# The last expert tile added to the residual on TensorE in PSUM, and the second-last tile's down products moved forward

## The reference

```python
x = x + mixer(rmsnorm(x))
lg = u @ router_group_w + b      # top-1 of 4 groups
le = u @ router_expert_w + b     # top-2 of the 4 experts of that group
h = silu(u @ expert_w_gate) * (u @ expert_w_up)      # 1024 -> 256, for each of 16 experts
x = x + einsum(h * combine, expert_w_down)           # 256 -> 1024
y = x * rsqrt(mean(x * x) + 1e-6) * final_norm_g
```

## Time and profile before

| | |
|---|---|
| time, median of 3 (lowest to highest) | 1022.35 us (1020.7 to 1022.99) |
| profiled execution: its own time, span | 1022.0 us, 1020.3 us |
| TensorE busy | 909.6 us, 89% of the span |
| VectorE, ScalarE, GpSimd busy | 407.5, 204.7, 37.0 us |
| mean granted clock of TensorE | 0.947 |
| last matmul ends, last scaling ends | about 996.75 us, 1017.42 us |

### The profile page before, as it was taken

How to read it: one execution, slowest core, us unless ns; L and a number is a source line. 1 busy time by engine, 2 the same in 40 slices (tenths; PEclk the granted TensorE clock), 3 DMA queues, 4 the chain that set the end, 5 groups by cost and what they waited for, 6 DMA issues and landing times. The chain is left out here.

```text
span 1020.3 us, 16857 instructions
## 1 busy us (share of the span) xinstructions
PE 909.6 (89%) x7262; PEld 631.3 (62%) x7262; DVE 407.5 (40%) x755; ACT 204.7 (20%) x403; POOL 37.0 (4%) x38
## 2 busy tenths in 40 slices
PE   5999999899999999899999999978899906999990
PEld 4777755777667777677777767755687702333330
DVE  3422145256369653543454454234731143121112
ACT  2100200013332132222122022213002140111113
POOL 0000000000000000000000000000000011222110
PEclk9999989699999999999999999969999957999996
DMA  9111101201211210100011100107352277999816
GB/s 356 66 63 62 62 27 49 101 12 51 92 53 44 71 32 33 32 14 31 33 33 43 43 23 23 42 1 260 127 228 82 76 302 302 394 379 390 310 30 199
DMA packets 26145, 116.53 MB, mean 114 GB/s; under 512 B 5016, under 2 KB 7320, under 8 KB 21208
## 3 DMA queue, kind: packets, MB, share of 16 engines
q1 hardware_dynamic: 21368, 102.28, 26.4%
q0 software_dynamic: 4704, 13.18, 4.7%
HBM read 102.76 MB, written 16.48 MB: 117 GB/s over the span
## 5 line engine op out<-in xcount | busy, mean ns | idle before, releaser
L757 PE MATMUL psum<-arena 128*128 128x268 f32 x1600 | 411.8, 405 | 8.1 <-ACT arena L1084 4.6
L757 PEld LDWEIGHTS psum<-arena 128*128 128x128 f32 x1600 | 295.8, 193 | 80.4 <-issue 9.8
L1263 DVE TENSOR_TENSOR arena<-psum,arena 128x512 f32<-128x512 f32 (+8 forms) x252 | 122.7, 488 | 278.8 <-PE psum L1023 55.8
L1084 ACT ACTIVATE arena<-psum 128x268 f32<-128x268 f32 (+7 forms) x166 | 68.8, 420 | 539.4 <-PE psum L757 324.5
L1263 DVE TENSOR_TENSOR arena<-arena 128x268 f32<-128x268 f32 (+11 forms) x221 | 109.4, 495 | 68.8 <-ACT arena L1084 57.8
L1023 PE MATMUL psum<-arena 128*128 128x268 f32 x384 | 91.3, 393 | 5.4 <-DVE arena L1263 5.4
L1726 PE MATMUL psum<-arena 128*32 128x512 f32 (+1 forms) x640 | 86.3, 602 | 2.9 <-DVE arena L1797 2.9
L1023 PEld LDWEIGHTS psum<-arena 128*128 128x128 f32 x384 | 71.7, 190 | 22.1 <-DVE arena L1263 7.5
L1797 DVE TENSOR_TENSOR arena<-psum,arena 128x256 f32<-128x256 f32 (+1 forms) x36 | 24.0, 691 | 117.6 <-ACT arena L1768 112.9
L1726 PEld LDWEIGHTS psum<-arena 128*32 128x32 f32 (+1 forms) x640 | 25.4, 116 | 61.5 <-issue 59.8
L1084 ACT ACT_TABLE_LOAD x36 | 46.2, 1283 | 39.9 <-PE psum L757 30.2
(11 more groups left out here) (162 smaller groups left out, 699.0 us busy)
## 6 DMA issues: line engine op xcount, KB each, us to landing
arena<-in_w_gu SPq DMA_DIRECT2D x16, 2048.0 KB, 15.3
arena<-in_w_in SPq DMA_DIRECT2D x46, 512.0 KB, 3.2
arena<-in_w_dn SPq DMA_DIRECT2D x16, 1024.0 KB, 15.3
arena<-in_w_out SPq DMA_DIRECT2D x2, 2048.0 KB, 13.7
arena<-in_x SPq DMA_DIRECT2D x8, 268.0 KB, 5.1
arena<-in_x SPq DMA_DIRECT2D x1, 2144.0 KB, 8.5
arena<-in_rets SPq DMA_DIRECT2D x1, 2048.0 KB, 16.7
out_rets<-arena SPq DMA_DIRECT2D x1, 2048.0 KB, 7.5
```

What stands on the lines that cost most here:

```text
L757: last = mm(ps, wt[:, i % NW, k, :], rhs[:, k, cols(hf)], start=(k == 0), stop=(k == nk - 1))
L1084: run(nc.scalar.activation(out, in_, fn, **kw), s)
L1263: run(v.tensor_tensor(out, a, b, op), s)
```

## The change

It has four parts, all in the last two tiles and the final norm.

1. The down products of tile 10 move into the middle of gate and up of tile 11, which is cut into pieces of 2, 2 and 4 contraction steps. Down now goes through one bank after the other (all four parts of bank 6, then bank 7).
2. Tile 11 is no longer read back out of DRAM with the others. SyncE starts the read-backs once the scatters of tiles 0 to 10 are in. GpSimd's scatter of tile 11 still happens, but waits for all five read-backs, and its end is waited for at the very end.
3. The sum x2 + tile 11 is made in PSUM. For each row tile t and each half q of 512 columns, `rest(t, q)` multiplies the identity with the read-back `xf`, and `added(t, q)` accumulates the product of a selection matrix `picks[:, t]` with `yo` on it. `picks[slot, t, row]` is 1 where the slot's row number is 128 t + row; VectorE makes it with five `tensor_scalar`. These are 20 matmuls. Three of the `rest` stand ahead of the transposes of tile 11. Row tile t uses banks 2t and 2t+1, modulo 8.
4. ScalarE loads the square root's table before it evicts tile 11, evicts it in two halves, and VectorE instead of ScalarE copies the transposes of tile 11. Squares and final scaling read PSUM instead of `xf`.

```diff
+        picks = at(TT * P, TT, P, start=ug0)
...
-                    for q in range(2):
-                        at_least(sp, q_yd[q], EVERY, EVERY)
+                    at_least(sp, q_yd[0], EVERY, EVERY)
+                    sp.nop(nofuse=True)
+                    at_least(sp, q_yd[1], EVERY, EVERY - 16)
...
+                    at_least(sp, q_yd[1], EVERY, EVERY)
...
+                        if e == NPASS - 1:
+                            for t in range(TT):
+                                at_least(pool, z_x[t], 16, 16)
...
+                    def rest(t, q):
+                        n = rows_of(t)
+                        if q == 0 and t < TT - 1:
+                            at_least(pe, z_x[t], 16, 16)
+                        if t == 2 and q == 0:
+                            at_least(pe, q_ws, 1, 1)
+                        mm(bank(2 * t % 8 + q, 512, n), ident[0:n, 0:n], xf[0:n, t, 512 * q:512 * q + 512],
+                           start=True, stop=False)
+
+                    def added(t, q):
+                        n = rows_of(t)
+                        if t == 0 and q == 0:
+                            at_least(pe, z_sel, 1, 1)
+                            at_least(pe, q_yh, 1, 1)
+                        if t == 0 and q == 1:
+                            at_least(pe, q_yo, NPASS, NPASS)
+                        if t == TT - 2 and q == 1:
+                            at_least(pe, z_x[TT - 1], 16, 16)
+                            at_least(pe, z_y, TT, 1)
+                        x = mm(bank(2 * t % 8 + q, 512, n), picks[:, t, 0:n],
+                               yo[:, (NPASS - 1) % 2, 512 * q:512 * q + 512], start=False, stop=True)
+                        if q:
+                            x.then_inc(z_sum, 1)
...
+                    gate_up(NPASS - 1, range(2))
+                    hidden_in(NPASS - 2)
+                    gate_up(NPASS - 1, range(2, 4))
+                    down(NPASS - 2)
+                    gate_up(NPASS - 1, range(4, KD))
+                    rest(0, 0)
+                    rest(0, 1)
+                    rest(1, 0)
+                    hidden_in(NPASS - 1)
+                    rest(1, 1)
+                    down(NPASS - 1)
+                    added(0, 0)
+                    rest(2, 0)
+                    added(0, 1)
+                    added(1, 0)
+                    added(1, 1)
+                    rest(2, 1)
+                    added(2, 0)
+                    added(2, 1)
+                    for t in range(3, TT):
+                        for q in range(2):
+                            rest(t, q)
+                        for q in range(2):
+                            added(t, q)
...
+                    e = NPASS - 1
+                    hidden_out(e - 1)
+                    rows_out(e - 1)
+                    gate(e)
                     a(dummy, eps2[:, :], ACT.Sqrt).then_inc(z_sq, 1)
+                    at_least(act, q_dh, 1, 1)
+                    at_least(act, q_yd[e % 2], EVERY, 16 * (e // 2))
+                    a(yo[:, e % 2, 0:512], bank(6), ACT.Copy, scale=w_s[:, e:e + 1]).then_inc(q_yh, 1)
+                    at_least(act, q_dn, NPASS, NPASS)
+                    a(yo[:, e % 2, 512:1024], bank(7), ACT.Copy, scale=w_s[:, e:e + 1]).then_inc(q_yo, 1)
                     for t in range(TT):
                         n = rows_of(t)
-                        at_least(act, z_x[t], 16, 16)
+                        at_least(act, z_sum, TT, t + 1)
                         if t:
                             at_least(act, z_ss, TT, t)
-                        a(junk[0:n], xf[0:n, t, :], ACT.Square, accum_out=fs[0:n, t:t + 1]).then_inc(z_ss, 1)
+                        a(junk[0:n], psum[0:n, 1024 * t % 4096:1024 * t % 4096 + 1024], ACT.Square,
+                          accum_out=fs[0:n, t:t + 1]).then_inc(z_ss, 1)
...
+                    e = NPASS - 1
+                    for t in range(TT):
+                        x = v.tensor_scalar(picks[:, t, :], cc("slot"), float(P * t - UNUSED), id_f[:, e:e + 1],
+                                            ALU.add, ALU.is_equal)
+                    x.then_inc(z_sel, 1)
+                    hidden(e)
+                    at_least(dve, q_ht, NPASS, NPASS)
+                    v.tensor_copy(hht.rearrange("p f t -> p (f t)"), bank(4, 256)).then_inc(q_hte, 1)
...
-                        v.scalar_tensor_tensor(yf[0:n, t, :], xf[0:n, t, :], fs[0:n, TT + t:TT + t + 1],
+                        v.scalar_tensor_tensor(yf[0:n, t, :], psum[0:n, 1024 * t % 4096:1024 * t % 4096 + 1024], fs[0:n, TT + t:TT + t + 1],
```

More of the change, by code:

```diff
@@ new lines, in _, with gate_up @@
+                    seen = [0, 0]
+                    def gate_up(i, ks):
+                        at_least(pe, q_ue, NPASS, i + 1)
+                        while seen[0] <= blocks(i)[-1][1]:
+                            x = seen[0]
+                            at_least(pe, s_we[x % NWE], loads_of(x % NWE), 16 * (x // NWE + 1))
+                            seen[0] += 1
+                        if i >= 2:
+                            at_least(pe, q_h, NPASS, i - 1)
+                        for k in ks:
+                            for part, x in blocks(i):
+                                last = mm(bank(2 + i % 2)[part], ue[:, i % 2, k, part], w_gu[x % NWE][:, k, :],
+                                          start=(k == 0), stop=(k == KD - 1))
+                        if k == KD - 1:
+                            last.then_inc(q_gu, 1)
@@ new lines, in hidden_in, with down @@
+                    def hidden_in(e):
+                        at_least(pe, q_h, NPASS, e + 1)
+                        if e:
+                            at_least(pe, q_hte, NPASS, e)
+                        for f in range(2):
+                            last = nc.tensor.transpose(bank(4)[:, P * f:P * f + P], hh[:, P * f:P * f + P], ident)
+                        last.then_inc(q_ht, 1)
+                    def down(e):
+                        at_least(pe, q_hte, NPASS, e + 1)
+                        while seen[1] <= blocks(e)[-1][1]:
+                            x = seen[1]
+                            at_least(pe, s_wd[x % NWE], loads_of(x % NWE), 16 * (x // NWE + 1))
+                            seen[1] += 1
+                        if e:
+                            at_least(pe, q_yo, NPASS, e)
+                        for q in range(2):
+                            for f in range(2):
+                                for part, x in blocks(e):
+                                    last = mm(bank(6 + q)[part], hht[:, f, part],
+                                              w_dn[x % NWE][:, f, 512 * q:512 * q + 512], start=(f == 0), stop=(f == 1))
+                            if q == 0 and e == NPASS - 1:
+                                last.then_inc(q_dh, 1)
+                        last.then_inc(q_dn, 1)
@@ new lines, in weights_in @@
+                    def weights_in():
+                        at_least(pe, q_wp, 1, 1)
+                        for j in range(2 * TT):
+                            last = mm(bank(5)[:, 3 * NPASS:6 * NPASS], onehot[:, j // TT, j % TT, :], w_pass[:, j],
+                                      start=(j == 0), stop=(j == 2 * TT - 1))
+                        last.then_inc(q_wsp, 1)
+                    def rest(t, q):
[6 more added lines that the diff above has]
+                           start=True, stop=False)
@@ new lines, in _ @@
+                    for i in range(NPASS - 1):
+                        gate_up(i, range(KD))
+                        if i == 0:
+                            weights_in()
+                        else:
+                            hidden_in(i - 1)
+                        to_channels(i + 1)
+                        if i:
+                            down(i - 1)
+                    gate_up(NPASS - 1, range(2))
+                    hidden_in(NPASS - 2)
+                    gate_up(NPASS - 1, range(2, 4))
@@ new lines, in rows_out @@
+                    def rows_out(e):
+                        at_least(act, q_dn, NPASS, e + 1)
+                        if e == 0:
+                            at_least(act, q_ws, 1, 1)
+                        if e >= 2:
+                            at_least(act, q_yd[e % 2], EVERY, 16 * (e // 2))
+                        a(yo[:, e % 2, :], psum[:, 3072:4096], ACT.Copy, scale=w_s[:, e:e + 1]).then_inc(q_yo, 1)
+                    for i in range(NPASS - 1):
+                        gate(i)
+                        if i:
+                            hidden_out(i - 1)
+                            rows_out(i - 1)
@@ L1855, in _, with hidden @@
                        ALU.mult, q_wp)
[L1856 to L1865, removed]
+                    def hidden(e):
+                        at_least(dve, q_sig, NPASS, e + 1)
+                        if e:
+                            at_least(dve, q_ht, NPASS, e)
+                        b = bank(2 + e % 2)
+                        tt(hh, b[:, 0:FF], sig, ALU.mult, q_h1)
```

(4 more changed lines are left out.)

73 lines of the change are left out of this document (15 added, 58 removed).

## The result

The changed kernel takes 1033.79 us (median of 4 runs, 1029.11 to 1036.63) against 1022.67 for the kernel before (4 runs, 1020.7 to 1025.7): a ratio of 1.0102 with a 95% interval of 1.0056 to 1.0147. It is slower. The forecast was 1030, between 1026 and 1035. The profiled execution took 1029.11 us with a span of 1027.4.

A forecast was written before the change was run, and what follows sets the result against it. TensorE bound the kernel until 996.75, then 20.7 us of latency. From 999.0, 21.15 us of TensorE work, 2.0 for the clock, 3.1 and 2.9 behind gave span 1028.2, 7.9 longer: 1030 us, range 1026 to 1035.

The forecast's parts named there:

- the forecast case: Whole kernel: the main outcome, slower, from 1027.5 to 1033 us, held at 72 in 100.
- Down 10 and gate and up 11: TensorE, reordered last tiles: down 10 ends at 987.51, 4.0 us earlier; gate and up 11 ends at 990.97.
- Scatter and read-back: Tile 10's scatter lands after 5.85 to 6.3 us, the first read-back 3.4 us after issue, near 999.0.
- The wait with tile 11 behind it: TensorE waits 8.0 us for x tile 0, with 3.95 us of tile 11's transposes and down queued behind.
- The clock: TensorE behind the wait: 4 us at half clock, a loss of 2.0 us.
- The added work: TensorE behind the wait: 20 products at 0.86 us, 17.2 us; with transposes and down 21.15 us at full clock.
- 1 (the read-back is there in time): TensorE, before the residual products: x tile 0 lands before 990.97, no wait, about 1020 us; 4 in 100.
- 2 (half price): TensorE's added products cost half, their two records overlapping: 8.6 us less, about 1022 us; 3 in 100.
- 3 (the clock does not fall): TensorE behind the wait: clock stays up or returns within a microsecond, 1028 us; 8 in 100.
- 4 (it stays low for 10 us and more): TensorE behind the wait: low clock for 10 to 17 us of work, 1033 to 1037 us; 10 in 100.
- 5 (exposed weight loads): TensorE's added products: 40 weight loads of about 0.2 us not overlapped, 8 us more, 1038 us; 3 in 100.
- the stores at the end: End of the kernel, behind the last scaling: the store adds 2.9 us.

The follow-up runs named there:

- e1: The changed kernel, unedited, timed again: 1033.87 us, ratio 1.0078 to the kernel before.
- e2: The changed kernel with transposes and down products of tile 11 ahead of all residual products: 1027.39 us, ratio 1.0028 to the kernel before.
- e3: The changed kernel with nine more float32 products, read by nobody, ahead of the first residual product: 1029.80 us, ratio 1.0055 to the kernel before.
- e8: e4 with down of tile 10 put back behind gate and up of tile 11: 1026.63 us, ratio 1.0017 to the kernel before.
- e4: The changed kernel with tile 11's transposes and down first, VectorE adding the residual of row tiles 0 to 3: 1020.90 us, 0.9959 of before.
- e9: e4 timed again, unedited: 1020.90 us, ratio 0.9979 to the kernel before.
- e11: e4 without GpSimd's last scatter of tile 11 and the wait for it: 1021.57 us, ratio 0.9976 to the kernel before.

## Why the prediction was right

**Direction and size.** Forecast: 7.9 us more. Measured: tails 8.6 to 9.5 us longer, ratios of 1.0078 and 1.0102, which are 8.0 and 10.4 us. The median of 1033.79 lies 4 us above the forecast of 1030; in profiles about one of these four is in the tail, the rest lies in stretches at half clock ahead of the change (e1), which the sum took from one execution of the kernel before. The range has no term for them; of the four timed executions one, 1036.63, is above its upper end of 1035, and that the median is inside by 1.2 us is in part luck. The sum for the low end of the forecast case is wrong too: a scatter of 5.85 us and 2.6 us at half clock give 1029.3, not 1027.5.

**Down 10 and gate and up 11.** Forecast to end 7.4 and 10.9 us behind the start of gate and up 11 in the chain. Measured from 978.25: 7.6 (985.81) and 11.1 (985.71 + 3.65 = 989.36). Right.

**Scatter and read-back.** 6.25 us and 3.56 us against 5.85 to 6.3 and 3.4. Right.

**The wait with tile 11 behind it.** 8.51 us against 8.0, 8.71 in the second profile. That it is a matter of the queue was argued from the order of instructions and is shown by e2.

**The clock.** 4.2 us at half (4.8 in e1) against the 4 taken between the rows at 850.9 and 142.4 of the earlier trace rows; e3 shows its price of 2.

**The added work.** 1.72 us for two products (four records) in the final stream, which is the 0.86 of the forecast. From 997.88 to 1021.62 are 23.7 us against 23.15: 0.3 more in the first three products (4.92 against 2.58 and the 2.0 for the clock), 0.2 at the switch to the first selection products (1.06 instead of 0.86) and 0.1 each in the last two groups, where the chain shows 1.82 and 1.84, and 0.15 less in the transposes.

**Rivals.** 1 (the read-back is there in time) falls with the 8.5 us. 2 (half price) falls with 1.72 us for four records. 3 (the clock does not fall) and 4 (it stays low for 10 us and more) fall with 4.2 and 4.8 us. 5 (exposed weight loads) would have shown 0.4 us more for each product; the stream shows none. The sentence of the Trainium skill ("TensorE: Matmul & The Clock Gate", section on packing small matmuls) that was weighed there does not describe these products: their loads of 0.19 us lie beside the 0.43 us records.

**The limit of the reasoning.** The sum gave the stores at the end as one latency, 2.9 us. That held for the changed kernel (2.83), but not for the variants, where stores, read-backs and the last scatter stand closer together (3.3 to 4.2).

## What to carry to other kernels

A wait belongs to everything that stands behind it in the same engine's list: three products with a wait for a DMA, put ahead of work that was ready, made an idle stretch of 8.5 us, and moving that work to the front took 6 us off, of which 2 were the clock. Before a step goes from a DMA to TensorE, compare what the path through the DMA takes (here 20.7 us from the last matmul to the last scaling) with the engine's full price in series (21 us of products, transposes and down at full clock); sharing the work with the idle VectorE made it pay, and only together with the earlier down of tile 10 (e8). And where whole runs differ by 5 us for reasons ahead of the edit, compare the stretch from the last common instruction to the end.

## What the runs showed of the hardware

The granted clock fell to half behind pauses shorter than the 3.55 us of the earlier trace rows: in the changed kernel before 992, at most 2.6 us after the last matmul (in e1 3.3), and in e4, e8 and e9 after pauses of 1.4 to 2.5 and 0.5 us, while in e2 and e11 pauses of 1.4 and 0.5 us left it at 1.00. So the length of the pause alone does not tell whether it falls. From one execution to another of one kernel whole stretches change their clock (1.00 or 0.54 near 260), and the times differ by up to 8 us, the longer ones at the lower mean clock.
